# A two-layer hybrid backbone on one Trainium2 core: retention scores and masks moved into the SSM output projection, modulation units into the qk units

## The reference, cut to what matters

```python
mod = (jax.nn.silu(cond) @ P['w_mod'][layer] + P['b_mod'][layer])[:, None, :]
...
# chunked_decay_scan, for each direction and chunk of 128 tokens
scores = jnp.einsum('bigd,bjgd->bgij', qc, kc)
y = jnp.einsum('bgij,bgrij,bjgrv->bigrv', scores, decay, vc)
y = y + jnp.einsum('bigd,bgrdv->bigrv', qc, s) * jnp.exp(cum)[..., None]
s = s * jnp.exp(last)[..., None] + jnp.einsum('bjgd,bjgrv,bgrj->bgrdv', kc, vc, w)
...
y_ret = head_layer_norm((ret_ys[0] + ret_ys[1])...)
y_ret = jax.nn.silu(g) * (y_ret * gn_gain)
out = jnp.concatenate([y_ret, y_ssm], axis=-1) @ w_out
```

## Time and profile before

| what | value |
|---|---|
| median of three runs | 1936.97 us |
| span of the profiled execution | 1940.2 us |
| PE busy | 1885.8 us, 97% |
| DVE busy | 1311.0 us, 68% |
| ACT busy | 864.2 us, 45% |
| POOL busy | 116.0 us, 6% |
| mean granted PE clock | 0.994 of full |
| PE's busy share, 552 to 604 us (retention loop) | 45.86 of 52 us |

### The profile page before, as it was taken

How to read it: one execution, slowest core, us unless ns; L and a number is a source line. 1 busy time by engine, 2 the same in 40 slices (tenths; PEclk the granted TensorE clock), 3 DMA queues, 4 the chain that set the end, 5 groups by cost and what they waited for, 6 DMA issues and landing times.

```text
span 1940.2 us, 33176 instructions
## 1 busy us (share of the span) xinstructions
PE 1885.8 (97%) x13269; PEld 1800.1 (93%) x13269; DVE 1311.0 (68%) x2131; ACT 864.2 (45%) x1473; POOL 116.0 (6%) x105
## 2 busy tenths in 40 slices
PE   7999999999998999999999999899999999999999
PEld 4998899999988999999999998866699999999999
DVE  5555956666777688788888877666547863663663
ACT  4645743222535366235335445555535641441551
POOL 0001200000010000000000035411100000000000
PEclk9999999999999999999999999999999999999999
DMA  8221014444322233432443331100013222222222
GB/s 313 87 69 44 18 61 131 137 146 154 97 76 74 79 109 119 141 125 99 145 129 116 101 101 59 46 12 1 1 55 108 84 70 74 76 68 84 73 69 75
DMA packets 57066, 175.96 MB, mean 91 GB/s; under 512 B 7552, under 2 KB 9472, under 8 KB 56832
## 3 DMA queue, kind: packets, MB, share of 16 engines
q1 hardware_dynamic: 55152, 172.17, 27.1%
q10 hardware_dynamic: 1808, 2.36, 0.4%
HBM read 170.05 MB, written 4.46 MB: 90 GB/s over the span
## 4 chain that ended last, share of the span: by engine, by line
PE 87%; DVE 6%; ACT 3%; issue 2%; DMA 1%; SPq 0%; POOL 0%; DVEq 0%; ACTq 0%
PE ps L392 74%; PE ps L2260 2%; PE ps L2245 2%; PE ps L982 1%; PE ps L2209 1%; PE ps L1417 1%; DVE w_lo L378 1%; DVE PT L2378 1%; DVE x L997 1%; PE ps L2208 1%; PE ps L1404 1%; DMA modw<-in_w_modA 1%; ACT yv L1864 1%; ACT w_hi L370 1%; PE ps L1428 1%
## 5 line engine op out<-in xcount | busy, mean ns | idle before, releaser
L370 ACT ACTIVATE w_hi<-raw 128x1024 fp32r<-128x1024 f32 (+1 forms) x221 | 230.4, 1043 | 585.8 <-PE ps L392 585.6
L378 DVE TENSOR_TENSOR w_lo<-raw,w_hi 128x1024 fp32r<-128x1024 f32 (+1 forms) x221 | 270.7, 1225 | 300.7 <-ACT w_hi L370 299.9
L392 PE MATMUL ps<-h_hi,w_hi 128*128 128x320 f32 x1392 | 322.4, 313 | 8.3 <-DVE x L997 3.0
L392 PE MATMUL ps<-h_lo,w_hi 128*128 128x320 f32 x1392 | 318.2, 310 | 2.8 <-DVE h_lo L785 1.6
L392 PE MATMUL ps<-h_hi,w_lo 128*128 128x320 f32 x1392 | 317.8, 310 | 0.0
L392 PEld LDWEIGHTS ps<-h_hi,w_hi 128*128 128x128 f32 x1392 | 231.1, 188 | 14.6 <-issue 4.9
L392 PEld LDWEIGHTS ps<-h_lo,w_hi 128*128 128x128 f32 x1392 | 232.9, 188 | 4.1 <-DVE h_lo L785 2.5
L392 PEld LDWEIGHTS ps<-h_hi,w_lo 128*128 128x128 f32 x1392 | 233.0, 188 | 0.0
L392 PE MATMUL ps<-ya_hi,w_hi 128*128 128x320 f32 (+1 forms) x896 | 207.6, 313 | 0.0
L392 PE MATMUL ps<-ya_hi,w_lo 128*128 128x320 f32 (+1 forms) x896 | 205.0, 310 | 0.0
L392 PE MATMUL ps<-ya_lo,w_hi 128*128 128x320 f32 x896 | 204.0, 309 | 0.0
(11 more groups left out here) (310 smaller groups left out, 3004.5 us busy)
## 6 DMA issues: line engine op xcount, KB each, us to landing
raw<-in_ffn_up SPq DMA_DIRECT2D x88, 512.0 KB, 3.5
raw<-in_hyb_in SPq DMA_DIRECT2D x49, 512.0 KB, 3.9
mrawB<-in_w_modB SPq DMA_DIRECT2D x48, 512.0 KB, 4.4
mrawA<-in_w_modB SPq DMA_DIRECT2D x64, 256.0 KB, 2.7
raw<-in_ffn_down SPq DMA_DIRECT2D x32, 448.0 KB, 3.4
raw<-in_hyb_out SPq DMA_DIRECT2D x16, 512.0 KB, 4.2
raw<-in_ffn_down SPq DMA_DIRECT2D x16, 512.0 KB, 3.6
modw<-in_w_modA SPq DMA_DIRECT2D x12, 512.0 KB, 12.8
```

The source lines that it names most:

```text
L370: act.activation(w_hi[:, i % 2, 0:n], raw[:, b % RAW, 0:n], ACT.Copy).then_inc(S("w_hi"), 1)
L378: eng.tensor_tensor(w_lo[:, i % 2, 0:n], raw[:, b % RAW, 0:n], w_hi[:, i % 2, 0:n].bitcast(F32), SUB).then_inc(S("w_lo"), 1)
L392: last = pe.matmul(pj(f, c1 - c0)[:, hh, :], w[:, i % 2, k * 128:(k + 1) * 128], v[:, k, c0:c1], start=(k == 0 and n == 0), stop=(k == s.K ...
```

## The change

Scores of all four pairs are computed inside wo_ssm: scores of pair p ahead of unit 4 + p, into banks that wo_ssm does not use (`RS`); states of pair 0 inside unit 7. DVE masks them behind units 3 to 6, into buffers free at that time (`PTr`), after the decay masks, now behind unit 2; the recurrence of pair 0 is there too, behind unit 6. ACT computes both decay masks behind unit 1, the state load goes behind unit 4. The loop keeps output, states and turns; the turn of head 2p-1 comes before the output of pair p+1, and the gates of head 2p-2 behind the recurrence. The six modulation units leave wo_ssm: qk units 0, 1, 3, 4 and 5 get two each, and g unit 6 (u = 22), which had none, gets unit 31.

```diff
-        PTr = nc.alloc_sbuf_tensor_at("PTr", [128, 2, NCH, 128], F32, offset=H0 + 6 * TOK * 4)
-        Sr = nc.alloc_sbuf_tensor_at("Sr", [128, 3, 2, 128], F32, offset=H0 + (KT + 6) * TOK * 4)
+        Sr = [t[:, :, :].rearrange("p a c -> p (a c)")[:, 1024:1280].rearrange("p (d v) -> p d v", d=2) for t in (u_sb, t_sb, hf2)]
+
+        def PTr(p, e):
+
+            if p < 2:
+                return yv[:, p, e, :, :]
+            return qkT[:, 2 * p + e, :].rearrange("p (c t) -> p c t", c=NCH)
...
+        TWICE = (0, 1, 3, 4, 5)
+        BEHIND = [u for u in range(-4, 23) for _ in range(2 if u in TWICE else 1)]
+        assert len(BEHIND) == 4 * QA
+
+        def half_after(i):
+
+            return BEHIND[i - 1] + 4 if i else -1
...
-                if units is not None and units + r < EARLY:
-                    dve_mod_unit(dve, units + r)
...
-                    if 8 * n + r < 22:
-                        dve_mod_unit(dve, 4 + 8 * n + r)
+                    for i, u in enumerate(BEHIND):
+                        if u == 8 * n + r:
+                            dve_mod_unit(dve, i)
...
+        RS = (TP, flat[:, 3072:3712].rearrange("p (c t) -> p c t", c=NCH))
...
-        def pe_ret_scores(pe, p, heads):
-
+        def pe_ret_scores(pe, p):
+
+            if p:
+                pe.wait_ge(S("ret_pt"), 2 * p)
+            else:
+                pe.wait_ge(S("tp_read"), tp_base["normS"] + 1)
+                pe.wait_ge(S("mod"), 5)
             for c in range(NCH):
-                for e in heads:
+                for e in range(2):
...
-                    if c == 0:
-                        pe.wait_ge(S("ret_pt"), h + 1)
-                    last = pe.matmul(R[e][:, c, :], PTr[:, e, c, :], vTM[:, c, 128 * h:128 * h + 128], start=True, stop=(c == 0))
+                    if c == 0 and p:
+                        pe.wait_ge(S("ret_yc"), h - 1)
+                    elif c == 0:
+                        pe.wait_ge(tp_read(stages["wo_ssm"], 6 + e), (stages["wo_ssm"].f0 + 6 + e) // 2 + 1)
+                    last = pe.matmul(R[e][:, c, :], PTr(p, e)[:, c, :], vTM[:, c, 128 * h:128 * h + 128], start=True, stop=(c == 0))
...
         def pe_ret(pe):
...
             for p in range(4):
                 pe_ret_out(pe, p)
                 if p < 3:
-                    pe_ret_states(pe, p + 1, range(0, 4))
-                    for e in range(2):
-                        pe.wait_ge(S("ret_yc"), 2 * p + e + 1)
-                        pe_ret_scores(pe, p + 1, (e,))
-                    pe_ret_states(pe, p + 1, range(4, 8))
-                    if p:
+                    pe_ret_states(pe, p + 1)
+                if p:
+                    pe_ret_turn(pe, 2 * p - 2)
+                    if p < 3:
                         pe_ret_turn(pe, 2 * p - 1)
+
+        def pe_wo_ssm(pe):
+            s = stages["wo_ssm"]
+            pe_first(pe, ((s, 0), (s, 1)), H, hready("normS"))
+            for r in range(2, 7):
+                if r >= 4:
+                    pe_ret_scores(pe, r - 4)
+                pe_unit(pe, s, r, 0, H)
+            pe_ret_scores(pe, 3)
+            pe_begin(pe, s, 7)
+            for k in range(KT):
+                if k == 5:
+                    pe_ret_states(pe, 0)
+                last = pe_tile(pe, s, 7, k, s.u0 + 7, s.f0 + 7, H)
+            last.then_inc(S("pe_unit"), 1)
...
+        def dve_ret_first(dve):
+            dve_ret_mask(dve, 3)
+            dve.wait_ge(S("ld_s0r"), 16)
+            dve_ret_recur(dve, 0)
+            dve.wait_ge(S("mod_part"), 8)
+            dve_ret_keep(dve, 0)
...
-            mask(0, 0)
-            mask(0, 1)
-            recur(0)
-            keep(0)
             for p in range(4):
+                stats(p, 0)
+                if p < 3:
+                    dve_ret_recur(dve, p + 1)
                 if p:
                     gates(2 * p - 2)
-                stats(p, 0)
-                if p < 3:
-                    mask(p + 1, 0)
-                    mask(p + 1, 1)
-                    recur(p + 1)
                 stats(p, 1)
...
-                        if b - (-1 if i < 26 else 1) == i and i < 4 * QA:
+                        while i < 4 * QA and b == half_after(i):
...
             act_out_stage(act, stages["wo_ssm"], None,
-                          {1: lambda: act_decay_masks(act, 0), 2: lambda: act_decay_masks(act, 1), 3: lambda: act_decay_rows(act),
-                           5: lambda: act_kw(act, 0), 6: lambda: act_state_load(act)})
+                          {1: lambda: act_decay_masks(act), 3: lambda: act_decay_rows(act),
+                           4: lambda: act_state_load(act), 5: lambda: act_kw(act, 0)})
...
-            dve_out_stage(dve, stages["wo_ssm"], gate(0, 2), None, 26, {6: lambda: dve_decay_masks(dve)})
+            dve_out_stage(dve, stages["wo_ssm"], gate(0, 2), None,
+                          {2: lambda: dve_decay_masks(dve), 3: lambda: dve_ret_mask(dve, 0), 4: lambda: dve_ret_mask(dve, 1),
+                           5: lambda: dve_ret_mask(dve, 2), 6: lambda: dve_ret_first(dve)})
```

More of the change, by code:

```diff
@@ L1672, in dve_ret_in, with act_decay_masks @@
                         dve_rstd(dve, "normS")
-                    if 8 * n + r < 22:
-                        dve_mod_unit(dve, 4 + 8 * n + r)
+                    for i, u in enumerate(BEHIND):
+                        if u == 8 * n + r:
+                            dve_mod_unit(dve, i)
         R = (flat[:, 1024:1664].rearrange("p (c t) -> p c t", c=NCH), flat[:, 0:640].rearrange("p (c t) -> p c t", c=NCH))
         KVR = flat[:, 3072:4096].rearrange("p (n v) -> p n v", n=8)
[L1680 to L1687, removed]
+        RS = (TP, flat[:, 3072:3712].rearrange("p (c t) -> p c t", c=NCH))
+        def act_decay_masks(act):
+            act.wait_ge(S("h_ready"), KT * (APPLIED.index("normS") + 1))
+            for d in range(2):
+                for h in range(RH):
+                    last = act.activation((mTf, mTb)[d][:, h, :], cst[:, (C_IJF, C_IJB)[d]:(C_IJF, C_IJB)[d] + 128], ACT.Exp,
+                                          scale=lrow[:, d * 8 + h:d * 8 + h + 1])
+                last.then_inc(S("ret_set"), 1)
         def act_decay_rows(act):
@@ L1747, in pe_ret_scores, with pe_ret_states @@
                         last.then_inc(S("ret_s"), 1)
-        def pe_ret_states(pe, p, slots=range(8)):
-            if slots[0] == 0:
-                pe.wait_ge(S("ret_kw"), p + 1)
-                if p:
-                    pe.wait_ge(S("ret_rec"), 6 * p)
-                    pe.wait_ge(S("ret_so"), p)
-            for n in slots:
+        def pe_ret_states(pe, p):
+            pe.wait_ge(S("ret_kw"), p + 1)
+            if p:
+                pe.wait_ge(S("ret_rec"), 6 * p)
+                pe.wait_ge(S("ret_so"), p)
+            else:
+                pe.wait_ge(S("ret_pt"), RH)
+            for n in range(8):
                 d, c = KV[n]
@@ L1789, in pe_ret_out @@
                         k = c - 2 if d == 0 else 3 - c
-                        state = s0r[rows, p, d, :] if k < 0 else Sr[rows, k, d, :]
+                        state = s0r[rows, p, d, :] if k < 0 else Sr[k][rows, d, :]
                         last = pe.matmul(R[e][:, c, :], qd[rows, d, c - 1, :], state, start=False, stop=(d == 1))
@@ L1880, in act_ret, with dve_ret_recur, dve_ret_keep, dve_ret_mask @@
             high(7)
+        def dve_ret_recur(dve, p):
+            dve.wait_ge(S("ret_kv"), p + 1)
+            for k in range(3):
+                for d in range(2):
+                    if k:
+                        dve.wait_ge(S("ret_rec"), 6 * p + 2 * (k - 1) + d + 1)
+                    prev = Sr[k - 1][:, d, :] if k else s0r[:, p, d, :]
+                    dve.scalar_tensor_tensor(Sr[k][:, d, :], prev, rtot[:, d, p:p + 1], KVR[:, 2 + 3 * d + k, :],
+                                             MUL, ADD).then_inc(S("ret_rec"), 1)
+        def dve_ret_keep(dve, p):
+            dve.tensor_copy(soutr[:, :, p, :], KVR[:, 0:2, :]).then_inc(S("ret_so"), 1)
+        def dve_ret_mask(dve, p):
+            if p == 0:
+                dve.wait_ge(S("ret_m"), 3)
+            for e in range(2):
+                dve.wait_ge(S("ret_s"), 2 * p + e + 1)
+                dve.tensor_tensor(PTr(p, e), RS[e], mTf[:, 2 * p + e:2 * p + e + 1, :].to_broadcast([128, NCH, 128]),
+                                  MUL).then_inc(S("ret_pt"), 1)
+        def dve_ret_first(dve):
[4 more added lines that the diff above has]
+            dve_ret_keep(dve, 0)
         def dve_ret(dve):
             n0 = KT * APPLIED.index("retT")
[L1885 to L1897, removed]
[L1898 to L1903 removed]
             def stats(p, e):
@@ L1952, in dve_ret @@
                 if p < 3:
-                    keep(p + 1)
-                elif p:
+                    dve_ret_keep(dve, p + 1)
+                else:
                     gates(2 * p - 1)
@@ L2599, in _ @@
             pe_ret_in(pe)
-            pe_stage(pe, stages["wo_ssm"], H, hready("normS"))
```

(1 more changed line is left out.)

27 lines of the change are left out of this document (4 added, 23 removed).

## The result

The changed kernel takes 1953.04 us (median of four, 1952.05 to 1956.01), the kernel before on the same chip 1937.2: ratio 1.0077, 95% interval 1.0064 to 1.0090, so slower by 15 us (12 to 17).

A forecast was written before the change was run, and what follows sets the result against it. PE was taken to bound the kernel nearly everywhere, the retention loop being a dependency chain with PE idle in pieces. Terms 0.5 + 6.1 + 9.6 - 1.1 - 4.0 - 0.7 = +10.4 us gave 1947.4, range 1936 to 1954.

The forecast's parts named there:

- Part 1 (a): qk units 0, 1, 3, 4, 5 with two modulation units each: DVE waits for half-buffer reloads; +0.5 us (0 to 4).
- Rival C: qk units: each of ten halves lands behind a weight load, 4.2 not 2.7 us; +14, 1951 us; chance 0.08.
- Part 1 (b): In front of normS: unit 31 with its flip delays the application, 5.1 us, plus 1.0 of clock loss; +6.1.
- Rival B: In front of normS: unit 31 costs nothing, something else holds the application; +4.3, 1941.3 us; chance 0.15.
- E: Rival B and Rival D together: unit 31 free and the loop at PE's pace; -6.5, 1930.5 us; chance 0.06.
- Part 2: In wo_ssm: scores 6.5, states 2.1, shape changes 1.0 us, all paid on PE; +9.6 us (7.6 to 12).
- Part 3: Start of the loop: first outputs 2.5 us sooner, 1.4 lost to clock after idling; net -1.1 (-2.5 to 0).
- Part 4: Retention loop: steps of 10.2, 12.3, 11.4 us gain 4.7, clock takes 0.7; net -4.0 (-12.6 to -2).
- Rival D: Retention loop falls to PE's pace, -12.6 us there and no idling; total -0.4, 1936.6 us; chance 0.12.
- Part 5: Start of wo_ret: PE idles 0.8 us instead of 2.4, half a clock loss goes; -0.7 (-1.5 to +0.3).

The follow-up runs named there:

- unit31_late: The changed kernel with modulation unit 31 moved from behind g unit 6 to behind wo_ssm unit 0; ratio 1.0043 to the kernel before, +8.3 us.
- mods_only: The kernel before with only the six modulation units moved as in the change, scores and masks staying in the loop; ratio 1.0050 to the kernel before, +9.7 us.
- warm: gates_first with 12 more small matmuls, results never read, in PE's wait between the loop and wo_ret; ratio 0.9988 to the kernel before.
- filler: spread with 15 more score matmuls, results never read, in PE's wait at the start of the loop; ratio 1.0021 to the kernel before.
- serial_heads: spread with the scores of a pair computed one head after the other; only one profiled execution, a block 2.16 us against 1.39 alternating.
- spread: The changed kernel with the six extra modulation units behind qk 1 and 4, v 2 and 5, g 0 and 3; ratio 1.0033 to the kernel before, +6.4 us.
- gates_first: states_behind with the gates of head 2p-2 ahead of the statistics of pair p; ratio 0.9998 to the kernel before.
- states_behind: spread with states of pair 0 behind wo_ssm's last unit and their recurrence behind the residual on DVE; ratio 1.0011 to the kernel before, +2.1 us.

## Why the prediction was right, and where not

**Direction and mechanism** held: unit 31 in front of normS, score blocks paid in full and a loop that gains less than they cost. The sizes owe something to luck. The 10.7 in the trace for 10.4 come from terms that were off by up to 2.2 us either way and evened out, and against a trace of before that had itself lost clock. The time is up by 15 us where 10.4 were forecast.

*Part 1 (a), doubled units*, was sized at +0.5 and is +2.7. The step that failed is "2.7 us to land": two of the halves landed after 3.4 to 3.5 us, and the slack worked out was 0.3 and 0.1 us. Why these two were slow is open: a weight load was issued 0.4 us behind the first of them, and none was under way at the second. The sum had the right two places, though behind qk 6 the wait was for the copy of the keys after the low split; it should have carried the spread of these landings (2.4 to 4.8 us over all halves in the trace of before) and not the median. Rival C had this mechanism at 4.

*Part 1 (b), unit 31*: 5.1 forecast, 5.1 found, and unit31_late shows that it goes with the unit's place. The clock's 1.0 did not come in this profile: the clock fell to 0.53 and 0.62 from 502 to 506, while PE waited for slices anyway. In mods_only it fell once more behind the wait and cost 1.5. The recorded reading of the earlier trace rows has a slip: at 0.147 us a record, 13.6 and not 16 fit into 2 us; the loss of 1.5 stands, as 19.8 against 18.2 us shows. Rival B is out, and E with it.

*Part 2*: 9.6 forecast, 8.2 found. The step that failed is the price of a block: 20 records take 1.32 us and not 1.62. The forecast divided L1791's 0.65 us by 8 records, 81 ns each, and scaled that to 20. But a block has a fixed part. From 8 records in 0.65 to 20 in 1.32 is 56 ns a record, with 0.2 left over in both; that 0.2 was scaled too. Blocks in one half of the rows show the same fixed part at half the pace: 24 records in 2.88 (warm) and 30 in 3.54 (filler), 0.11 a record and 0.2 over. In the traces the records of one half start 111 to 112 ns apart, and those of alternating heads start in pairs, 112 ns from pair to pair. serial_heads shows that the alternation makes the difference. The tiling rule of the Trainium skill (TensorE: Matmul & The Clock Gate, Part 3) lets the time fall to half of one-after-the-other, an estimated 1.05. The trace agrees in the pace, which is half; the measured 1.32 is above the estimate by the fixed part. Around a block, the change of shape cost 0.10 at each side, as taken. All that was to hide did: no wait of PE between wo_ssm units 2 and 7.

*Part 3*: -1.1 forecast, +0.3 found. The wait was right (3.28), the clock's share was not: 2.7 us for 1.4. The size came from a stretch of dense unit matmuls after 2.4 us of idle; the clock stayed low longer here, from 577 to 584, with windows like this one:

```profile
578.00:580.00 2.00, 2.00 (x12) 1.78 (x12) 0.00 (x0) 0.00 (x0) 0.00 (x0) 0.50 0.00 0
```

Behind the same wait the loss was 1.4 in serial_heads, 2.7 in the changed kernel and 4.2 in spread and unit31_late: a term with a range of 1.4 to 4.2, which I had put at one value. What decides between them is open.

*Part 4*: -4.0 forecast, -4.3 found; steps 10.1, 12.0 and 12.2 for 10.2, 12.3 and 11.4. In the last, PE and not ACT ended last: the clock had fallen to 0.50 after its 2 us wait. The near hit is partly luck. 1.3 of the 4.3 is the clock that the last step of before had lost; against the same loop at full clock, in mods_only (38.0 from first copy to wo_ret), the new loop gains 2.9. Rival D had to have copies 9 apart; they never came below 9.9.

*Part 5*: -0.7 forecast, -1.3 found, and the size says little: this stretch is 19.8 in the first profile of before and 18.2 in the second, 18.5 in the changed kernel. Where PE had idled 2.37 us in front of it, it took 19.8 (before, mods_only, gates_first); where PE had idled 0.8 or less, 18.2 to 18.5 (the nine others). The mechanism holds, but before itself may or may not pay it.

**What stays open.** The table's 10.7 is not the 15 of the timed runs. Part of the gap is arithmetic. The prediction put the profiled execution of before 3.2 us above the median, by comparing its span with times. Every execution with both on record has a time 1.8 to 1.9 us above its span (1952.82 and 1951.0 in the changed kernel), so that execution took an estimated 1942.0, 4.8 to 5.0 above the median. The spans differ by 10.8; with 4.8 more that is the difference of the medians. So the forecast was made against an unusually long execution of before.

How much of the 15 us is the clock's is not settled by single profiles. Over the 16 executions of before beside the first experiments, time follows the mean granted clock, from 1935.79 us at 0.998 to 1944.26 at 0.992, with a median of 0.995; the changed kernel's four have 0.990 to 0.991. At that slope, 1.4 us for 0.001, an estimated 6 of the 15 us go with the clock.

Part of that lies outside the stretch. The changed kernel is 2.8 us later at qk 0 already, in code that both share; the windows of 20 to 30 us show the clock there, first before, then after:

```profile
20.00:30.00 10.00, 9.85 (x99) 5.96 (x100) 4.67 (x11) 7.17 (x13) 0.00 (x0) 0.92 1.03 406
```

```profile
20.00:30.00 10.00, 9.81 (x88) 6.72 (x87) 2.34 (x7) 5.19 (x9) 0.00 (x0) 0.62 1.03 408
```

The same lateness, 2.2 and 2.0 us, is in the profiles of mods_only and unit31_late, which share its modulation order, and in no other with more than 1.0. Whether that is chance or has a cause in the build was not tried. Against it, the stretch behind wo_ret's third unit was 1313.7 to 1313.8 us in five of the profiles and 1315.3 to 1316.6 in the other seven, with the granted clock at 0.89 to 0.94 from 1230 to 1260 us in the seven and 1.00 in the five, the changed kernel among them. So single profiles of this kernel carry 2 to 3 us of clock that no edit tried here accounts for.

## What to carry to other kernels

When filler work is moved between stages, look at what each queue does at the new place: work behind the last split before a dependent stage is paid in full, and two pieces that share a buffer in one iteration pay the buffer's reload. Work moved from a loop that another engine's chain holds into a stage that the bound engine fills gains only what the chain loses; here 8.2 us of PE bought 5.6, and 2.6 of these were clock that the profile of before had lost. Put it into a wait of that engine instead, which here paid twice: 2.1 us of states in PE's wait (states_behind) brought the first copy 6.2 us forward, by the time and by the clock. When a short block is priced from a row, take two blocks of different length, or the fixed part is scaled with the rest. And before terms of one or two microseconds are read from a pair of profiles, profile the kernel before twice.

## What the runs showed of the hardware

- 15 useless small matmuls in a 3.3 us wait of PE made the kernel 4.1 us faster up to the first copy in the trace; 12 in a 2.4 us wait gave 1.2 us. Without them the clock went to 0.50, its 1.2 GHz level, behind such a wait, and held there through 3 to 10 us of work.
- fp32 products of 64 rows start 112 ns apart, record by record, in one half of the array's rows; where they alternate between the halves, two start in that time. A block of either kind has some 0.2 us on top, and standing between 128-row matmuls another 0.10 at each side.
- Of 256 KB half loads issued one behind the other at DVE's pace, some took 3.4 to 3.5 us to land and not 2.7.
- The same program (the kernel before) took 1935.8 to 1944.3 us in 16 executions, and the time went with the mean granted clock, 0.998 to 0.992.
